# Attention stage of a decoder block: each engine's work sorted by a position of its own per kind of work, in place of common steps

## What is computed

```
s_c = einsum('bqgrd,bjgd->bgrqj', q, kcmp) - slopes*dist_c      # compressed keys
p_c = softmax(where(mask_c, s_c, NEG_INF)) * mask_c
o_cmp = einsum('bgrqj,bjgd->bqgrd', p_c, vcmp)
imp = einsum('bgrqj,jk->bgqk', p_c, overlap)                    # importance of 32 key blocks
_, sel_idx = lax.top_k(where(forced, 1e6, imp), 8)              # 8 blocks of 64 keys chosen
s = q . ks[chosen] - slopes*dist; p = softmax(s); o_sel = p @ vs
sw = q . kw[last 512] - slopes*dw; pw = softmax(sw); o_win = pw @ vw
o = gate0*o_cmp + gate1*o_sel + gate2*o_win
```

## Time and profile before

| | us |
|---|---|
| three runs | 4177.17, 4173.85, 4180.6 (median 4177.17) |
| the profiled execution | 4168.6, of which the span of the instructions is 4166.9 |
| attention stage (what the change touches) within the span | 1593 to 2492 |
| its start-up / long tiles / short tiles / last units | 1593 to 1635 / to 2130 / to 2450 / to 2492 |

### The profile page before, as it was taken

One profiled execution on the slowest core, in us unless ns is written; L12 is line 12 of the kernel. 1 busy time (PEld: TensorE's weight loads), 2 busy tenths in 40 slices (PEclk: granted clock), 3 DMA queues, 4 the chain that ended last, 5 costly groups with the idle time before them and its releaser, 6 DMA issues. The chain is left out here.

```text
span 4166.9 us, 70072 instructions
## 1 busy us (share of the span) xinstructions
PE 3817.1 (92%) x26880; PEld 3148.6 (76%) x26881; DVE 2347.5 (56%) x3712; ACT 2020.5 (48%) x3225; POOL 725.5 (17%) x1297
## 2 busy tenths in 40 slices
PE   7899999999998968999998968999599999999798
PEld 5777777777776746888877757999488888887687
DVE  2555555565556525766665636444676445567565
ACT  2433433344333315777776753222376555566565
POOL 1111111211112112333333530000111000001120
PEclk9999999999999878999999979999699999999899
DMA  4534433443333332000000006332497666679642
GB/s 130 154 101 111 135 101 98 131 124 101 105 93 90 79 95 60 19 14 19 14 21 19 25 25 208 122 122 97 178 350 292 234 242 242 234 299 376 246 151 94
DMA packets 512857, 557.23 MB, mean 134 GB/s; under 512 B 106189, under 2 KB 374477, under 8 KB 511533
## 3 DMA queue, kind: packets, MB, share of 16 engines
q1 hardware_dynamic: 479988, 461.10, 35.0%
q0 software_dynamic: 16416, 59.78, 3.8%
q10 hardware_dynamic: 16176, 32.55, 2.1%
HBM read 439.78 MB, written 113.57 MB: 133 GB/s over the span
## 5 line engine op out<-in xcount | busy, mean ns | idle before, releaser
L555 PE MATMUL fr_fb<-fr_hT_h,fr_w_h 128*128 128x512 f32 (+1 forms) x1312 | 535.1, 408 | 11.1 <-ACT fr_zs L836 7.6
L555 PE MATMUL fr_fb<-fr_hT_r,fr_w_h 128*128 128x512 f32 (+1 forms) x1312 | 531.1, 405 | 0.0
L555 PE MATMUL fr_fb<-fr_hT_h,fr_w_r 128*128 128x512 f32 (+1 forms) x1312 | 531.0, 405 | 0.0
L1005 DVE TENSOR_TENSOR fr_w_r<-fr_w_raw,fr_w_h 128x1024 fp32r<-128x1024 f32 (+1 forms) x164 | 199.0, 1214 | 499.1 <-ACT fr_w_h L809 498.1
L2121 DVE TENSOR_TENSOR aq_p_lo<-aq_t_bank,aq_p_hi 128x512 fp32r<-128x512 f32 (+1 forms) x420 | 283.9, 678 | 234.6 <-ACT aq_p_hi L2045 230.0
L836 ACT COPY fr_zs<-fr_fb 128x512 f32<-128x512 f32 (+1 forms) x148 | 87.1, 589 | 510.2 <-PE fr_fb L555 509.7
L555 PEld LDWEIGHTS fr_fb<-fr_hT_h,fr_w_h 128*128 128x128 f32 (+1 forms) x1312 | 248.1, 189 | 79.3 <-ACT fr_zs L836 13.3
L2045 ACT CAST aq_p_hi<-aq_t_bank 128x512 fp32r<-128x512 f32 (+1 forms) x420 | 237.4, 574 | 135.7 <-PE aq_t_bank L1949 129.1
L555 PEld LDWEIGHTS fr_fb<-fr_hT_h,fr_w_r 128*128 128x128 f32 (+1 forms) x1312 | 248.3, 189 | 63.3 <-issue 10.9
L555 PEld LDWEIGHTS fr_fb<-fr_hT_r,fr_w_h 128*128 128x128 f32 (+1 forms) x1312 | 248.7, 190 | 62.4 <-issue 11.0
L134 PE MATMUL ex_gu<-wx_gate_w,ex_xT 128*128 128x512 f32 x1176 | 288.3, 401 | 4.6 <-DVE ex_xT L2904 4.6
(11 more groups left out here) (499 smaller groups left out, 8950.4 us busy)
## 6 DMA issues: line engine op xcount, KB each, us to landing
wk_raw<-in_w_exp_gate_up SPq DMA_DIRECT2D x64, 2048.0 KB, 9.6
fr_w_raw<-in_w_in SPq DMA_DIRECT2D x160, 512.0 KB, 3.9
wk_raw<-in_w_exp_down SPq DMA_DIRECT2D x32, 2048.0 KB, 10.4
s_z<-fr_zs SPq DMA_DIRECT2D x160, 256.0 KB
s_rows<-ex_y ACTq DMA_DIRECT2D x50, 512.0 KB, 4.4
mx_mg<-s_z SPq DMA_DIRECT2D x32, 512.0 KB, 7.5
fr_zc<-s_z SPq DMA_DIRECT2D x15, 903.0 KB, 6.6
sh_shared<-in_x SPq DMA_DIRECT2D x16, 512.0 KB, 5.3
```

The costliest lines, as they stand in the source:

```text
L555: ins = pe.matmul(bank[0:cols_, :], (w_h, w_h, w_r)[p][:, k, c, 0:cols_].bitcast(F32R), (hT_h, hT_r, hT_h)[p][:, c, :].bitcast(F32R), star ...
L1005: dve.tensor_tensor(w_r[:, m % 2, :, 0:cols_].bitcast(F32R), w_raw[:, m % 2, :, 0:cols_], w_h[:, m % 2, :, 0:cols_], ALU.subtract).then_in ...
```

## The change

The steps are gone as loops. Each engine gets one list, sorted by a number: the step as before plus an offset for that kind of work on that engine. There are two tables of offsets, `LONG` and `SHORT`, chosen by whether the step lies before the first block of unit (7, 0, WIN), block 278. `turn(n)`, `hi(n)` and `lo(n)` stand at n itself. Scores are spread over fractions of steps (`/` for `//`) between bounds from a third table, `SPREAD`. The number of instructions of each kind stays the same, and so do the buffers and, but for the constants in them, the waits. The kind `turn` of a front is now called `turn_p`. Of the tables a line each stands here.

```diff
-    Y_RING, FRONTS_APART, TABLE_STEPS, TURN_BEHIND, TURN_LATER = 3, 7, 8, 5, 1
+    Y_RING, FRONTS_APART, TABLE_STEPS = 3, 7, 8
+    LONG = {"pe": {"weigh": 2.35, "score": 0.3, "scores": -10.05, "turn_p": -3.25, "out": -0.25, "back": 2.45, "turn_y": 5.95},
+            "act": {"exp": 2.1, "exps": -8.15, "turn_p": -3.05, "out": -0.1, "back": 2.25, "turn_y": 5.25, "take": 1.95},
...
-                    step = max(begin + i * max(end - begin, 1) // len(runs), self.taken(u, h, at, wide) - 1)
+                    step = max(begin + i * max(end - begin, 1) / len(runs), self.taken(u, h, at, wide) - 1)
...
+        def put(step, kind, *what, engines, latest=None):
+            for engine in engines:
+                at = step + (self.LONG if step < cut else self.SHORT)[engine][kind]
+                orders[engine].append((at if latest is None else min(at, latest), len(orders[engine]), kind, *what))
...
+            put(out, "exps", t, g, engines=("act",))
+            put(out, "select", t, g, engines=("dve",))
+            put(out, "choose", t, g, engines=("pool",))
+            put(max(self.begin[self.at[t, g, SEL]], out + 6), "bias", t, g, engines=("pool",))
...
+            put(f[u + 1], "back", t, 2 * g + b, engines=("pe", "act"))
+            put(f[u + 1] - 1, "take", u, engines=("act",))
...
+                if run[5]:
+                    put(step, "exp", *run[:5], engines=("act",), latest=self.needed(run[1], run[2]) - 0.1)
+        self.pe, self.act, self.dve, self.pool = ([what[2:] for what in sorted(orders[engine])] for engine in ("pe", "act", "dve", "pool"))
...
-                for n in STEPS:
-                    if 0 <= n < F.n:
-                        turn(n)
-                    if 0 <= n - 2 < F.n:
-                        weigh(n - 2)
-                    for what in F.pe.get(n, ()):
-                        event(*what)
-                    for i, u, h, at, wide, last in F.runs_at.get(n, ()):
-                        score(i, u, h, at, wide)
+                for kind, *what in F.pe:
+                    if kind == "turn":
+                        turn(*what)
...
-                def take_out(n, u):
-                    act.wait_ge(pv_made, n - 1)
+                def take_out(u):
+                    act.wait_ge(pv_made, F.first[u + 1])
```

More of the change, by code:

```diff
@@ L1306 @@
 class Plan:
-    Y_RING, FRONTS_APART, TABLE_STEPS, TURN_BEHIND, TURN_LATER = 3, 7, 8, 5, 1
+    Y_RING, FRONTS_APART, TABLE_STEPS = 3, 7, 8
+    LONG = {"pe": {"weigh": 2.35, "score": 0.3, "scores": -10.05, "turn_p": -3.25, "out": -0.25, "back": 2.45, "turn_y": 5.95},
+            "act": {"exp": 2.1, "exps": -8.15, "turn_p": -3.05, "out": -0.1, "back": 2.25, "turn_y": 5.25, "take": 1.95},
+            "dve": {"mask": 0.1, "scores": -10.1, "inverse": -8.1, "select": 0.25, "totals": 1.2},
+            "pool": {"normalise": -3.6, "add_heads": -2.9, "open": -0.15, "choose": 2.35, "bias": -2.7, "add": 2.7, "take_q": -0.05}}
+    SHORT = {"pe": {"weigh": 2.35, "score": 0.7, "scores": -9.55, "turn_p": -4.3, "out": -0.65, "back": 2.3, "turn_y": 5.4},
+             "act": {"exp": 1.7, "exps": -8.6, "turn_p": -4.35, "out": -0.55, "back": 2.4, "turn_y": 5.65, "take": 2.5},
+             "dve": {"mask": 0.2, "scores": -10.05, "inverse": -8.5, "select": 2.4, "totals": -0.6},
+             "pool": {"normalise": -7.35, "add_heads": -2.8, "open": -0.05, "choose": 3.85, "bias": -1.45, "add": 2.2, "take_q": 1.4}}
+    SPREAD = {"first_from": 0, "first_to": -0.1, "second_from": -0.1, "second_to": 3.4, "local_from": 2.8, "local_to": -0.25, "short_local_from": -0.2, "short_local_share": 0.57, "short_after": 1.1, "short_before": 2.25}
     def __init__(self):
@@ L1366, in __init__, with put_block @@
+        def put_block(engine, step, kind, n):
+            orders[engine].append((step, len(orders[engine]), kind, n))
+        for n in range(self.n):
+            put_block("pe", n, "turn", n)
+            put_block("act", n, "hi", n)
+            put_block("dve", n, "lo", n)
+            put(n, "weigh", n, engines=("pe",))
         for n, (t, g) in enumerate(pairs):
             out = self.out_step[n]
-            marks += [(out - 10, 0, n, "scores", t, g), (out - 4, 1, n, "turn", t, g), (out, 2, n, "out", t, g)]
@@ L1369, in __init__ @@
-            marks += [(out - 9, 0.3, n, "exps", t, g), (out - 7, 0.6, n, "inverse", t, g), (out + 3, 2.5, n, "select", t, g)]
-            pool += [(out - 6, 0, n, "normalise", t, g), (out - 3, 0.5, n, "add_heads", t, g), (out, 2, n, "open", t, g),
-                     (out + 4, 0.7, n, "choose", t, g), (max(self.begin[self.at[t, g, SEL]] - 2, out + 4), 1, n, "bias", t, g)]
+            put(out, "scores", t, g, engines=("pe", "dve"))
+            put(out, "exps", t, g, engines=("act",))
+            put(out, "inverse", t, g, engines=("dve",))
@@ L1394, in __init__ @@
+        self.misc = {}
+        for kind, *what in self.pe:
+            if kind in ("scores", "turn_p", "out", "back", "turn_y"):
+                self.misc[kind, what[0], what[1]] = len(self.misc)
+        for before, after in zip(pairs, pairs[1:]):
+            assert self.misc["turn_p", *before] < self.misc["scores", *after] and self.misc["out", *before] < self.misc["turn_p", *after]
         for t, g in pairs:
@@ L2000, in event @@
                         ins.then_inc(cexp_ok, 1)
-                    if kind == "turn":
+                    if kind == "turn_p":
                         act.wait_ge(misc_made, n + 1)
```

122 lines of the change are left out of this document (60 added, 62 removed).

## The result

The changed kernel takes 4076.31 us (median of 4 runs, 4069.96 to 4084.65) beside 4175.51 of the kernel before on the same chip (4 runs, 4167.23 to 4180.6): 0.9766 of it, 95% interval 0.9752 to 0.978. Run once more on another chip it took 4073.26 (5 runs), 0.9767 (0.9746 to 0.9788). So the gain is 99 us.

What follows compares the result with a forecast made beforehand. TensorE, busy 92%, was taken as the bound, with about 101 us idle in the stage. Gains 6 + 5.5 + 5 + 3 + 5 + 3.5 + 3 = 31 us, less 7, gave 24: 4177.2 - 24 = 4153 us, range 4129 to 4180.

Steps and rivals of the forecast that it cites:

- 5.5 + 5 + 3: Long tiles: gains of 5.5 us from five fronts, 5 from the other waits for `lo`, 3 from `take` ahead of `hi`.
- new waits: Waits the new order may add, such as a mask ahead of its block's `lo`: 7 us lost, between 0 and 20.
- rest: Long tiles: 14.2 us in 27 waits for `lo` outside the costly fronts; a third, 5 us, was to go.
- Start: 6: Start of stage: earlier table removes a 3.62 us wait, scores fill 2.4 of 6.0 idle; 6 us, between 3 and 8.
- Short tiles: 5: Short tiles: `back` waits less for ScalarE's copy of `out`, 9.3 us before; gain 5 us, between 0 and 9.
- Last units: 3.5: Last units: `back` ahead of `weigh` saves 0.98 us at three ends, partly at one more; 3.5 us, between 3 and 4.
- Clock: 3: TensorE's granted clock, half speed behind a 2.10 us wait: 3 us gained of some 21 at most, between 0 and 8.
- Rival 1: Whole stage: waits only move, as buffers stay tight; only start and end gain, about 4172 us; chance 0.18.
- Rival 2: VectorE stands at `select` for GpSimd with `lo` behind it: 4185 us, 4195 if short tiles join; chance 0.13.
- Rival 3: More than the sum: clock's 21 us and the long waits' 14.2 all come, 45 us gained, 4132; chance 0.08.
- the marks set down for the profile after: Signs if right: 3.62 us wait gone, `lo` about 14, `back` for `out` about 4, `back` behind `take`, stage about 875.

## Why the prediction was wrong, point by point

**The sign and the mechanism of the long tiles were right, their size was not.** The terms for them, 5.5 + 5 + 3, less a share of the new waits, come to some 10 us; idle time there fell by 23.1. The 9.7 us of waits around 1771 to 1914 went whole, where 5.5 were counted, and of the "rest" more than a third went: the wait for `lo` fell from 23.9 to 7.1 us and not to 14.

**The step that failed.** The sum priced a few named waits of TensorE and took every other edit at nothing. It priced `exp` by the six waits around 1771 to 1914 and a third of the rest, and did not read that ScalarE stood 54.4 us at masks; undoing `exp` costs 51 us. It priced `score`, `mask`, `weigh` and the spread at nothing, apart from the start and `weigh` in the last units, where undoing them costs 42 and 37 us. And it sized the short tiles by one row of their waits, 5 us for 26.2 of idle time, and the clock at 3 for 22.

**Start: 6, measured 4.5.** The stage starts 4.7 us later in this trace, so times are to be read from its start: the table is made from 22.7 us on, where it was 33.2, and is done after 26.3, as foretold (1620 is 26.9 us behind the start of before). The mask that waited 6.39 us no longer waits; VectorE comes to it behind other work 32.6 us after the start, where it was 37.0. TensorE's wait of 3.62 us did not go whole but became 1.31:

```profile
1618.44 0.10 POOL L1876 MEMSET aq_imp<- 128x1 f32 x1
...
1620.50 3.62 POOL L1913 TENSOR_TENSOR aq_tg<-sh_shared,aq_sel 128x2048 f32<-128x2048 f32 x1
...
1630.41 1.22 DVE L2140 CUSTOM_DVE_ANT_0 aq_sc_odd<-aq_s_bank,aq_tg 128x1024 f32<-128x1024 f32 x1
...
1631.78 0.47 PE L1995 MATMUL aq_s_bank<-at_k_hi,at_q_s 128*128 128x512 f32 x1 [1.31 <-DVE aq_least L2140]
```

**Short tiles: 5, measured 41.8 in length.** This is the term that failed most. It looked at one kind of wait, `back` for the copy of `out`, which did go (9.3 us to 0.3). But idle time fell by 26.2 us: `back` behind two other small results went with it (5.6 and 3.6 us, above), and the waits for `take`, which the prediction said would stay at 6.6, fell to 4.2. The other 15.6 are about what the clock gives at most, half of the 34.1 us at half clock.

**Last units: 3.5, measured 4.6.** A little over its range of 3 to 4, and by the step named: `back` stands directly behind `take`, and `weigh` behind it.

**Clock: 3, measured 22.** The bound was about right, "some 21 us", worked out from PEclk by stretch. The choice within it was wrong: it showed one stretch behind one wait of 2 us, and 3 us is what two such stretches cost. In the short tiles the clock fell behind waits of 1.1 us as well, and these went too. The Trainium skill, TensorE: Matmul & The Clock Gate, section A second HAM failure mode: psum-queue depth-cycling, tells of a kernel in which frequent short idles between groups of matmuls make the clock go back and forth between its levels. The short tiles of before agree with that: 34.1 us at half clock with one wait over 1.5 us. The kernel with 97 short waits put in does not bear it out: one stretch in the middle.

**New waits: −7, measured near nothing.** `back` for `take` is the only new row of size, 10.4 us in 13 over the stage, and it stands for 19.3 us in 24 of `weigh`.

**The rivals.** Rival 1 (waits only move) fell: 59 us of idle time went with the same buffers. The Trainium skill, Perfetto Trace Analysis, section Optimization Strategy (the prediction names the section before it), says that the same gap coming again can mean too little room. In this kernel it did not: 33 waits for `lo` became 9 by order alone. Rival 2 fell: the view of the changed kernel shows no wait of VectorE for GpSimd in the stage. Rival 3, to which the prediction gave 0.08, was the nearest, and still 56 us too high: it had the whole of the clock's 21 us and of the 14.2 us of waits for `lo`, but left the short tiles at 5. Its sum does not come out either: 24 us with 21 for 3 and 14.2 for 5 is 51 and not 45, that is 4126, below the prediction's own range.

Of the marks set down for the profile after, the missing 2 us waits in the long tiles and `back` behind `take` came as foretold, and the wait of 3.62 us in part. The wait for `lo` (14 foretold, 7.1), `back` for `out` (4, 0.3) and the stage (875, 807.4) all erred to one side: here a sum of a few priced waits came to a quarter of the gain. The first paragraph of the prediction had the 101 us of TensorE's idle time, of which 59.0 went.

## What to carry to other kernels

Where one engine is busy nine tenths of the time, the idle time of the engines that feed it does cost something when a piece that it needs is queued behind the waiting one; so read what each feeding engine waits for, with what stands behind the wait, and not the bound engine's waits alone.

Change order on all engines together, and do not add up what the pieces give one by one: here `exp` and the scores' group put back at once cost 133 us and apart 93, three other groups together 52 and apart 100, and one kind moved to where its own waits vanish gained nothing, because another engine then waited.

And take TensorE's clock as a term of its own, from the granted clock by stretch, with the whole of what lies there as its upper end: in the middle of this stage all of it came back, though most of it did not stand behind long waits.

## What the runs showed of the hardware

A wait does not set the clock by its length alone. In the kernel before the same wait of a transposition comes four times, 2.10, 2.20, 1.91 and 2.23 us, up to 1774.57, 1810.95, 1845.23 and 1880.06. The clock fell behind the first and the last. Behind the second, 2.20 us, it did not (the wait, and the stretch behind it with the columns as above, PEclk 1.00):

```profile
1810.95 0.66 PE L1949 MATMUL aq_t_bank<-at_ident,aq_sc_odd 128*128 128x128 f32 x4 [2.20 <-DVE aq_p_lo L2121]
```

```profile
1811.00:1814.40 3.40, 3.40 (x27) 3.19 (x28) 3.40 (x8) 1.31 (x3) 1.04 (x1) 1.00 0.00 0
```

In the kernel with long waits put in 24 blocks the clock fell behind six waits, of 1.74 to 3.24 us, and stayed up behind one of 1.87 and another of 1.74; in the kernel before it fell behind single waits of 1.1 us in the short tiles, and in the changed kernel waits of 1.1 to 1.3 us left it at 1.00. Nor does the sum of idle time tell: in the short tiles 23.3 us of it went with none at half clock (`weigh`, `score` and `mask` undone) and 23.2 us with 20.5 (`exp` undone, where each of the four falls stands behind a wait of 1.83 to 2.46 us). What decides stays open.

Between start and last units the falls lasted 3.4 or 6.8 us, one of them 10.2 (`exp` and score undone). At the stage's start the clock differs between two executions of one kernel: the one with the 25 idle matmuls had 12.6 us at half clock there in its first trace and 21.7 in its second, and its start took 33.8 and 37.1 us, so a few us of a stage can be the clock alone. And matmuls that nobody needs hold the clock up through a chain of waits (0.89 and 0.79 over the last units in two traces, for 0.61), which here was worth 2 to 4 us of the stage and nothing that the whole time shows.
